# Loads of a decoder step's page compression placed in the mLSTM stage: first pages, sample states and block weights ahead, second pages at the opening

## What is computed

```python
def nsa_compress(kb, w1, w2, pe):
    nc = T // CMP_BLK
    blk = kb.reshape(B, nc, CMP_BLK, G, D) + pe[None, None, :, None, :]
    flat = jnp.moveaxis(blk, 3, 2).reshape(B, nc, G, CMP_BLK * D)
    return jax.nn.gelu(flat @ w1) @ w2
```

## Time and profile before

| | us |
|---|---|
| median of 3 runs | 2445.17 |
| lowest and highest run | 2442.57, 2445.93 |
| the profiled execution | 2449.38 |
| its span, first to last instruction | 2447.70 |
| mean granted TensorE clock, as a share of 2.4 GHz | 0.959 |

### The profile page before, as it was taken

How to read it: one execution, slowest core, us unless ns; L and a number is a source line. 1 busy time by engine, 2 the same in 40 slices (tenths; PEclk the granted TensorE clock), 3 DMA queues, 4 the chain that set the end, 5 groups by cost and what they waited for, 6 DMA issues and landing times. The chain is left out here.

```text
span 2447.7 us, 40582 instructions
## 1 busy us (share of the span) xinstructions
PE 2274.5 (93%) x15929; PEld 2076.1 (85%) x15929; DVE 1076.7 (44%) x2444; ACT 694.8 (28%) x1396; POOL 417.5 (17%) x380
## 2 busy tenths in 40 slices
PE   8999985887898989999899999999999999999996
PEld 7799964774565669999899968899999999999996
DVE  2214355126667671132227124367554554552336
ACT  4212052104656651011233013443111111121123
POOL 0000021321332311212001100111211211222220
PEclk9999987888999989999999999999999999999998
DMA  4211113987543431111311245221111111111312
GB/s 142 94 48 44 31 2 116 288 266 278 170 132 128 140 132 52 57 39 52 114 44 35 96 180 207 65 64 64 56 52 44 44 52 44 42 42 42 115 43 80
DMA packets 114154, 228.80 MB, mean 93 GB/s; under 512 B 23378, under 2 KB 76275, under 8 KB 110572
## 3 DMA queue, kind: packets, MB, share of 16 engines
q1 hardware_dynamic: 88106, 178.97, 22.3%
q0 software_dynamic: 10368, 28.33, 3.7%
q10 hardware_dynamic: 15490, 18.91, 2.3%
HBM read 202.91 MB, written 27.45 MB: 94 GB/s over the span
## 5 line engine op out<-in xcount | busy, mean ns | idle before, releaser
L88 PE MATMUL psum<-x_half_high,ff_half 128*128 128x352 f32 x3240 | 790.8, 324 | 10.8 <-POOL ff_half L69 4.9
L88 PEld LDWEIGHTS psum<-x_half_high,ff_half 128*128 128x128 f32 x3240 | 567.0, 189 | 12.8 <-POOL ff_half L69 5.9
L88 PE MATMUL psum<-h_again_low,ff_half 128*128 128x352 f32 x1176 | 378.0, 321 | 0.0
L69 POOL TENSOR_TENSOR ff_half<-ring,ff_half 128x1024 fp32r<-128x1024 f32 (+2 forms) x85 | 177.2, 2085 | 752.4 <-ACT ff_half L3082 752.4
L88 PEld LDWEIGHTS psum<-h_again_low,ff_half 128*128 128x128 f32 x1176 | 222.0, 189 | 0.0
L3082 ACT ACTIVATE ff_half<-ring 128x1024 fp32r<-128x1024 f32 (+2 forms) x88 | 78.0, 888 | 428.7 <-PE psum L88 406.6
L88 PE MATMUL psum<-merged_high,oq_half 128*128 128x352 f32 x768 | 189.9, 328 | 9.3 <-DVE oq_half L69 7.7
L88 PE MATMUL psum<-mid_low,ff_half 128*128 128x352 f32 x516 | 167.0, 324 | 0.0
L88 PEld LDWEIGHTS psum<-merged_high,oq_half 128*128 128x128 f32 x768 | 136.1, 191 | 9.9 <-DVE oq_half L69 8.0
L88 PE MATMUL psum<-x_half_high,mg_w_high 128*128 128x352 f32 x384 | 124.0, 323 | 2.0 <-ACT gated L2154 1.2
L88 PE MATMUL psum<-h_again_low,mg_w_high 128*128 128x352 f32 x384 | 123.1, 321 | 0.0
(11 more groups left out here) (560 smaller groups left out, 4224.6 us busy)
## 6 DMA issues: line engine op xcount, KB each, us to landing
na_kv<-in_pool SPq DMA_DIRECT2D x128, 128.0 KB, 3.6
na_kv<-in_pool POOLq DMA_DIRECT2D x128, 128.0 KB, 4.0
sab_kv<-in_pool SPq DMA_DIRECT2D x96, 128.0 KB, 4.6
mg_w<-in_w_merge SPq DMA_DIRECT2D x15, 768.0 KB, 4.3
sab_kv<-in_pool POOLq DMA_DIRECT2D x88, 128.0 KB, 4.7
ring<-in_f_wu SPq DMA_DIRECT2D x22, 512.0 KB, 3.5
ring<-in_f_wg SPq DMA_DIRECT2D x22, 512.0 KB, 3.6
sab_kv<-in_pool ACTq DMA_DIRECT2D x72, 128.0 KB, 6.1
```

The source lines that it names most:

```text
L69: return engine.tensor_tensor(low, x, high.bitcast(F32), ALU.subtract)
L88: ins = nc.tensor.matmul(out, w[a], x[b], start=first and n == 0, stop=last and n == 2)
```

## The change

- In the mLSTM stage qT and kt are placed first, and together they take exactly the bytes of the buffer for sequence 0's pages. When the last from_state has read qT and the last weighing has read kt, SP loads all 32 pages of sequence 0, in two batches of 16; each batch is read as page numbers first and then issued. The second batch and then the three final stores stand behind the first on SP.
- SP also loads w1 near the start of this stage, and C0 after the convolution's stores.
- In the next stage, SP, ACT and POOL load sequence 1's pages at the opening, in steps of three pages on each of the three queues, without a wait; `pairs` and some small tiles are moved to memory that no page buffer covers. On ACT turn_pairs now stands ahead of its page loads, and the loads of sequence 1 behind the gelu calls are gone.
- Waits on PE and the counts of the page semaphores follow.

```diff
 def mlstm(...)
+        qT, kt = sb("qT", [P, MH, TP]), sb("kt", [P, NTILE, MH, MD])
+        assert nc.sbuf_base == N["kv_at"] + 4 * NPAGE * 2 * PAGE
+        kT = sb("kT", [P, MH, TP])
...
-            sp.dma_start(O["p_mconv"], zm[:, :, TP - 3:TP]).then_inc(S["stored"], 16)
+            sp.dma_start(O["p_mconv"], zm[:, :, TP - 3:TP]).then_inc(S["conv_kept"], 16)
+            sp.dma_start(N["w1"][:, :, :, :], A["cmp_w1"]).then_inc(N["w1_ahead"], 16)
             sp.wait_ge(S["staged"], 4)
             sp.dma_start(O["s_mconv"], xs[:, :, :, TS:TS + 3]).then_inc(S["stored"], 16)
+            sp.wait_ge(S["conv_kept"], 16)
+            sp.dma_start(N["C"][:, :, :, :], A["s_C0"]).then_inc(N["C_ahead"], 16)
+            for at in range(0, NPAGE, 16):
+                page = [sp.value_load(pages[0:1, e:e + 1], min_val=0, max_val=N["n_pool"] - 1) for e in range(at, at + 16)]
+                if at == 0:
+                    sp.wait_ge(S["inter_ready"], NTILE)
+                    sp.wait_ge(S["kw_ready"], NTILE)
+                for e, g in zip(range(at, at + 16), page):
+                    sp.dma_start(N["kv"][:, e, :], A["pool"][ds(g, 1), :, 0:2 * PAGE].rearrange("a p x -> (a p) x")
+                                 ).then_inc(N["kv_ahead"], 16)
             sp.wait_ge(S["finished"], 3)
             sp.dma_start(O["p_C"], Ct[:, :, :]).then_inc(S["stored"], 16)
             sp.dma_start(O["p_n"], cn[:, :]).then_inc(S["stored"], 16)
             sp.dma_start(O["p_m"], mc[0:1, NTILE, :]).then_inc(S["stored"], 16)
-            sp.wait_ge(S["stored"], 80)
+            sp.wait_ge(S["stored"], 64)
 def states_and_blocks(...)
-            step = count if n else 3
+            step = count if n > 1 else 3
...
-                if n == 1:
-                    eng.wait_ge(S["own1_ready"], 2)
...
         def _(sp):
-            sp.dma_start(w1[:, :, :, :], A["cmp_w1"]).then_inc(S["w_loaded"], 16)
             sp.dma_start(w2[:, :, :], A["cmp_w2"]).then_inc(S["w_loaded"], 16)
             sp.dma_start(rel[:, :], A["rel"]).then_inc(S["vec_loaded"], 16)
-            load(sp, 0, 0, SP_N, loaded)
+            load(sp, 1, 0, SP_N, loaded)
             sp.wait_ge(S["qk_ready"], 1)
             sp.dma_start(onehot, A["onehot"]).then_inc(S["vec_loaded"], 16)
-            sp.dma_start(C[:, :, :, :], A["s_C0"]).then_inc(S["C_loaded"], 16)
-            load(sp, 1, 0, SP_N, loaded)
...
         def _(pool):
-            for n in range(NSEQ):
+            for n in range(1, NSEQ):
                 load(pool, n, SP_N + ACT_N, POOL_N, loaded_soft)
...
             def own_first(kv):
                 if kv == 0:
-                    pe.wait_ge(S["w_loaded"], 32)
+                    pe.wait_ge(N["w1_ahead"], 16)
                     pe.wait_ge(S["pe_loaded"], 32)
                     pe.wait_ge(S["turned_pairs"], 8)
...
             def first(n, kv):
-                if kv == 0:
+                if kv == 0 and n == 0:
+                    pe.wait_ge(N["kv_ahead"], 16 * NPAGE)
+                elif kv == 0:
...
             act.dma_start(m0[:, :], A["s_m0t"]).then_inc(S["small_loaded"], 16)
-            load(act, 0, SP_N, ACT_N, loaded)
             turn_pairs(nc.scalar.copy, 1)
+            load(act, 1, SP_N, ACT_N, loaded)
             act.wait_ge(S["qk_ready"], 1)
...
-            load(act, 1, SP_N, ACT_N, loaded)
             for n in range(NSEQ):
                 gelu(n, 0)
```

More of the change, by code:

```diff
@@ L492, in _, with mlstm @@
                     convolve(j - 4)
+W1_AT = 221152
 def heads_weights(ring):
     return ring[:, 0, :].rearrange("p (j h d) -> p j h d", j=2, h=MH)
-def mlstm(nc, A, O, K, zm, hm, cw, wqk, tokm, tokn, sm, psum):
+def mlstm(nc, A, O, K, N, zm, hm, cw, wqk, tokm, tokn, sm, pages, psum):
     lf, b, a, g = sm["lf"], sm["b"], sm["a"], sm["g"]
@@ L522, in mlstm @@
         sq = sb("sqs", [P, MH, MD])
-        names = ("loaded", "staged", "conv_steps", "conv_ready", "silu_done", "steps", "gate_sig", "cum_ready",
+        assert nc.sbuf_base <= W1_AT
+        names = ("loaded", "conv_kept", "staged", "conv_steps", "conv_ready", "silu_done", "steps", "gate_sig", "cum_ready",
                  "og_done", "og_scaled", "ones_set", "q_ready", "k_ready", "q_copied", "k_copied", "kt_ready", "kt_copied",
@@ L892, in block_views, with states_and_blocks, sb @@
             "vc": t[:, kc + NSEQ * P:BLOCKS_W].rearrange("p (n b) -> p n b", n=NSEQ)}
-def states_and_blocks(nc, A, O, K, N, zn, hm, tokm, sm, pages, ring, tile_at, spare, c_at, psum):
+def states_and_blocks(nc, A, O, K, N, zn, hm, tokm, sm, pages, ring, tile_at, spare, psum):
     NB = PAST // CB
     with stage(nc, "sab") as (ctx, sem):
-        sb = lambda n, s: ctx.enter_context(nc.sbuf_tensor("sab_" + n, s, F32))
-        kv_in = [sb(f"kv{b}", [P, NPAGE, 2 * PAGE]) for b in range(2)]
-        kv1_at = nc.sbuf_base - 4 * NPAGE * 2 * PAGE
+        assert nc.sbuf_base == N["kv_at"]
+        top = N["kv_at"] + 4 * NPAGE * 2 * PAGE
+        def sb(n, shape):
+            nonlocal top
+            t = tile_at("sab_" + n, shape, top)
+            top += -(-4 * int(np.prod(shape[1:])) // 32) * 32
+            return t
+        kv_in = [N["kv"], sb("kv1", [P, NPAGE, 2 * PAGE])]
         NPR = TP // 2
-        pairs = tile_at("sab_pairs", [P, 2, 2, NPR + CB // 2], kv1_at)
         place, limit = spare
@@ L915, in dead @@
             return t
-        w1, w2, pb = dead("w1", [P, 2, CB // 2, HD]), dead("w2", [P, 2, P]), dead("pb", [P, 8])
+        w1, C = N["w1"], N["C"]
+        w2, pb = dead("w2", [P, 2, P]), dead("pb", [P, 8])
+        pairs = dead("pairs", [P, 2, 2, NPR + CB // 2])
         act_out, act_own = dead("act", [P, 2, 2, P]), dead("act_own", [P, 2, NCMP])
@@ L965, in load, with loads_before @@
                                   ).then_inc(done[n % 2], 16)
+        def loads_before(n):
+            return sum(1 for m in range(1, n + 1) if m % 2 == n % 2)
         def turn_pairs(copy, kv):
@@ L1044, in first @@
             def first(n, kv):
-                if kv == 0:
-                    pe.wait_ge(loaded[n % 2], 16 * (SP_N + ACT_N) * (n // 2 + 1))
-                    pe.wait_ge(loaded_soft[n % 2], 16 * POOL_N * (n // 2 + 1))
+                if kv == 0 and n == 0:
+                    pe.wait_ge(N["kv_ahead"], 16 * NPAGE)
+                elif kv == 0:
+                    pe.wait_ge(loaded[n % 2], 16 * (SP_N + ACT_N) * loads_before(n))
+                    pe.wait_ge(loaded_soft[n % 2], 16 * POOL_N * loads_before(n))
                 if n == 0:
@@ L1075, in from_state @@
             def from_state(heads):
-                pe.wait_ge(S["C_loaded"], 16)
+                pe.wait_ge(N["C_ahead"], 16)
                 for h in heads:
@@ L3578, in build @@
         with ExitStack() as c:
-            mlstm(nc, A, O, K, zm, hm, cw, heads_weights(ring), tokm, tokn, sm, psum)
             N = {"n_pool": A["pool"].shape[0],
                  "soft": {n: ctx.enter_context(nc.semaphore(n)) for n in ("c0", "c1", "n0", "n1")}}
+            N.update({n: ctx.enter_context(nc.semaphore(n)) for n in ("w1_ahead", "C_ahead", "kv_ahead")})
             tile_at = lambda name, shape, at: nc.alloc_sbuf_tensor_at(name, shape, F32, offset=at)
+            N.update(kv_at=nc.sbuf_base, kv=tile_at("first_pages", [P, NPAGE, 2 * PAGE], nc.sbuf_base),
+                     w1=tile_at("block_w1", [P, 2, CB // 2, HD], W1_AT), C=tile_at("sample_C", [P, NSEQ, MH, MD], place["low"] + 4 * 4 * T))
+            mlstm(nc, A, O, K, N, zm, hm, cw, heads_weights(ring), tokm, tokn, sm, pages, psum)
             N.update(block_views(tile_at("blocks", [P, BLOCKS_W], place["tokm"])))
             states_and_blocks(nc, A, O, K, N, zn, hm, tokm, sm, pages, ring, tile_at,
-                              (place["tokm"] + 4 * BLOCKS_W, place["tokm"] + 4 * NTILE * (C_OG + 512)), place["low"] + 4 * 4 * T, psum)
+                              (place["tokm"] + 4 * BLOCKS_W, place["tokm"] + 4 * NTILE * (C_OG + 512)), psum)
         early.close()
```

14 lines of the change are left out of this document (7 added, 7 removed).

## The result

| | before | after |
|---|---|---|
| median of 9 runs each, us | 2445.63 | 2453.20 |
| lowest and highest, us | 2441.38, 2450.12 | 2450.77, 2456.99 |
| the profiled execution, us | 2449.38 | 2456.99 |
| its span, us | 2447.70 | 2455.30 |

The ratio of after to before is 1.0034, with a 95% interval of 1.0024 to 1.0044, that is 5.9 to 10.8 us. Forecast were 2453.9 us and slower by 8.7.

The account below looks back on a forecast made before the run. PE, busy for 93% of the span, was taken as the bound, with time won or lost mostly where it stands still. Terms 8.4 + 0.5 − 0.2 = +8.7 us gave 2453.9 us; the 8-in-10 range was 2447.0 to 2458.5.

Parts of the forecast that it names:

- SP's list: Before the mLSTM stage's end barrier: SP's page issues and number reads delay the three final stores by 8.4 us.
- The landing of the stores: At the barrier: final stores land later with pages in front of them, +0.5 us, between 0 and 2.2.
- The opening: Start of the next stage: bias_part(0) 2.0 us earlier, 1.8 given back at low clock; net −0.2 us, −2.9 to +1.4.
- The page loop: Next stage's page loop: costed at nothing, since earlier loading of sequences 0 and 1 frees no buffer sooner.
- The sum: Whole kernel: 8.4 + 0.5 − 0.2 = +8.7 us, giving 2453.9 us.
- Bound by transport, hence faster: Rival on the next stage: full DMA engines bound it, so moving loads gives −6.0 us, 2439.2 us; chance 0.09.
- The no-change case: Rival: opening shortens by own_first(0)'s whole 9.6 us, needing an early one-hot table or fitting second batch; 2444.5 us, chance 0.15.

Follow-up runs that it names:

- experiment 1: Changed kernel with all 32 page numbers read in one batch in SP's idle time, then all 32 pages issued: 2443.95 us, ratio to before 1.0002.
- experiment 3: Changed kernel with sequence 0's pages on two queues, SP issuing pages 0 to 15 and GpSimd the rest: 2441.98 us, ratio to before 0.9983.
- experiment 4: Changed kernel with SP waiting until all 32 pages of sequence 0 have landed before the three final stores: one execution, 2457.68 us.
- the two pairs of profiles: Kernel before and changed kernel, both unchanged, each profiled twice: spans 2447.7 and 2433.4 us before, 2455.3 and 2453.4 after.
- experiment 6: Changed kernel with sequence 0's pages on SP and GpSimd, one-hot table after three pages, ScalarE's page loads behind its gelu calls: 2433.01 us, ratio to before 0.9953.
- Experiment 8: Two-queue kernel with early one-hot table and late ScalarE loads, ScalarE's page numbers also read one gelu earlier: 2433.75 us, against 2433.01 without that.
- 2: Changed kernel with the three final stores issued ahead of the second batch's 16 pages: 2447.67 us, ratio to before 1.0023.

## Why the prediction was right

- **SP's list, +8.4 us.** Measured 8.5 (stores at 411.64 against 402.60, less 0.5 of drift). Taking the reads away gives back 9.2 us with what the stores land sooner (experiment 1), and sharing the issues too gives back all 11.1 (experiment 3). Shown.
- **The landing of the stores, +0.5 us.** This is the mis-sized term. From the last store's issue to s the changed kernel takes 4.3 us in both profiles, the kernel before 1.9: +2.4, just above the bound of 2.2. I placed it "nearest to the quiet case" though no row of before had a store behind pages. The pages did land in quiet time (median 2.4 us for the 32), but the very last one took 4.2 us, to 415.5, and SP left at 416.5. The rule on completion order in the Trainium skill ("DMA: Bandwidth & Descriptors", Queues, rings and completion order) spoke for a larger value. The trace agrees in kind: the stores do not end before the last page has landed, and with the pages landed first 4.3 falls to 2.6 (experiment 4).
- **The opening, −0.2 us.** In the two pairs of profiles first(0,0) moves by −0.3 and by +0.7 us against s, on average by +0.2. bias_part(0) came at s + 20.7 and s + 20.0, where 20.7 was forecast, and at the low clock (granted 0.50 from 437 to 447 us), 1.12 us as against 0.65. That the place was met is luck: two errors cancel. The one-hot table was issued at s + 14.6 and not at s + 17.0, because SP's page issues began 3.2 us sooner after s than before, where the forecast took off only the 0.5 us of w1's issue; and it was used 6.1 us later (5.4 in the second profile), where 3.7 was forecast with an upper bound of 5.3. Scores came at s + 14.6 and not at s + 18.4, which changed nothing, since PE then waited for the table. That own_first(0) starts 9.5 us earlier was worth nothing, since scores and the one-hot table wait; experiment 6 shows that these two were the holders.
- **The page loop, 0 us.** 113.4 and 112.1 us before, 113.3 and 114.1 after. The number was right; the reason given, that only freed buffers release loads, is incomplete. Experiment 8 speaks for transport as the pace there, but over the pages of sequences 3 to 7, and the change takes none of these away.
- **The sum.** By the first pair of profiles the stage of states and blocks ends 11.2 us later, of which 0.5 came from earlier stages: 10.7 us against a forecast of 8.7. The second pair gives 13.9, because the second profile of the kernel before has a stage 3 us shorter. The ratio of the runs says 8.3, with 5.9 to 10.8. The barrier alone makes 11.1, just above that interval. The kernels of experiments 1, 2 and 3 show the same gap: the barrier makes +1.9, +8.0 and 0 us there, and the ratios say +0.5, +5.6 and −4.2. So the kernels with early loads are 1 to 4 us faster than these terms say, twice beyond the interval. No profile shows where, since spans scatter more than that, and the cause is open. That the forecast lies near the middle of the interval is therefore partly luck: the landing was put 1.9 us too low, and some 3 us of gain were not forecast.
- **The rivals.** "Bound by transport, hence faster" did not happen. The no-change case needed, among its two conditions, SP's second batch to fit before the tail ends; experiment 1 makes it fit and measures 1.0002.

## What to carry to other kernels

A load that is moved into an earlier stage is hidden only if the list of the engine that issues it is done before that stage's other engines are: count its issues (0.52 us here) and its register reads (0.56 us), and what stands behind them, such as stores that a barrier waits for. Read indices before the wait that releases the batch, and give the issues to a queue that is idle. And look at what holds the stage that is to be shortened before its data are moved: here a small table and one engine's place in the order held it, and early data showed a gain in that stage only after these were out of the way.

## What the runs showed of the hardware

C0's load, issued in the mLSTM stage, took 5.00 us to issue and 29.8 us to land, where it took 9.4 us in the full queues of the next stage before the change; w1 took 10.7 instead of 5.2. The rows of the changed kernel, by issue (KB each, median us to landing), and the window:

```profile
sample_C<-in_s_C SPq DMA_DIRECT2D x1, 2048.0 KB, 29.8
...
block_w<-in_cmp_w SPq DMA_DIRECT2D x1, 1024.0 KB, 10.7
...
300.00:325.00 25.00, 21.56 (x80) 11.90 (x81) 11.26 (x61) 15.20 (x21) 0.15 (x1) 0.93 1.18 67
```

The DMA engines are shown as full (1.18) at 67 GB/s. The kernel before has 0.49 in that window for 15 GB/s. By the program the convolution states are loaded and stored there in pieces of 12 bytes, so it may be that the large transfers queue behind them; no run takes these pieces away, and the reason is not shown. It costs no wait here: C0 has landed at 340.2, and PE first uses it at 458.39. That small stores take 2.4 us longer behind pages which themselves land in 2.4 us was not expected either; the last 1.7 us before SP leaves pass with all DMA engines silent.
